# Attention pipeline of a decoder trunk: order of the copies and the scalings, and ScalarE making the upper half of each collected chunk

## What is computed

```python
s = jnp.einsum('bqhd,bkhd->bhqk', qi, k).astype(jnp.float32) * scale
p = masked_softmax(s, (kpos[None, :] <= qpos[:, None])[None, None])
return jnp.einsum('bhqk,bkhd->bqhd', p.astype(v.dtype), v)
...
out = gt[..., 0:1] * o_c + gt[..., 1:2] * o_s + gt[..., 2:3] * o_w
```

## Time and profile before

| what | us |
|---|---|
| median of the runs | 1398.74 |
| the profiled execution's own time | 1394.51 |
| its span, first to last instruction | 1392.5 |
| attention of the first layer | from about 141.5 to 251.8 |
| attention of the second layer | from about 773.4 to 882.6 |

### The profile page before, as it was taken

The page is one execution under the profiler, slowest core; times in us unless marked ns, Lnnn a source line. Parts: engine busy times, 40 slices in busy tenths (PEclk is TensorE's granted clock), DMA queues, the critical chain, the costliest instruction groups (busy, mean ns, idle before and its releaser), DMA issues.

```text
span 1392.5 us, 24791 instructions
## 1 busy us (share of the span) xinstructions
PE 1322.3 (95%) x10397; PEld 827.9 (59%) x10457; DVE 972.9 (70%) x1305; ACT 680.5 (49%) x970; POOL 151.9 (11%) x134
## 2 busy tenths in 40 slices
PE   7999898999999999999999989998999999999992
PEld 4357444444444444444356445458988988988981
DVE  7986676586650356334895675567888889989996
ACT  6245665253220132212245665347476677777772
POOL 0010331330000000031010120230400000000003
PEclk9999999999999999999999999999999999999997
DMA  8330883235320244003331100209899999999985
GB/s 314 106 91 16 275 295 116 98 130 180 138 91 0 96 176 167 1 16 141 127 91 31 31 1 1 65 14 369 319 376 373 339 357 393 369 369 391 364 312 198
DMA packets 39997, 255.49 MB, mean 183 GB/s; under 512 B 5626, under 2 KB 6778, under 8 KB 25418
## 3 DMA queue, kind: packets, MB, share of 16 engines
q1 hardware_dynamic: 30490, 220.00, 42.1%
q0 software_dynamic: 8960, 33.26, 7.2%
q10 hardware_dynamic: 432, 0.59, 0.1%
HBM read 218.08 MB, written 33.65 MB: 181 GB/s over the span
## 4 chain that ended last, share of the span: by engine, by line
PE 82%; issue 5%; DVE 5%; ACT 3%; DMA 3%; POOL 1%; SPq 0%; DVEq 0%; POOLq 0%; ACTq 0%
PE bank L1117 19%; PE bank L1118 19%; PE bank L1119 18%; PE bank L1338 4%; PE bank L1355 3%; PE bank L1385 2%; ACT arena L1655 2%; DVE small L2084 2%; PE bank L678 1%; PE bank L680 1%; PE bank L679 1%; PE bank L668 1%; PE bank L670 1%; PE bank L669 1%; DMA expert_slots<-arena,row_index 1%
## 5 line engine op out<-in xcount | busy, mean ns | idle before, releaser
L928 DVE SCALAR_TENSOR_TENSOR arena<-arena 128x3072 f16<-128x3072 f32 x86 | 288.3, 3352 | 11.0 <-ACT arena L782 10.9
L782 ACT ACTIVATE arena<-arena 128x3072 f16<-128x3072 f32 x86 | 237.9, 2767 | 42.2 <-DMA arena<-in_ew 23.3
L1117 PE MATMUL bank<-arena 128*128 128x144 bf16 (+3 forms) x893 | 218.9, 264 | 5.7 <-DVE arena L928 3.0
L1118 PE MATMUL bank<-arena 128*128 128x144 f16 (+3 forms) x894 | 219.2, 264 | 1.2 <-DVE arena L1842 1.2
L1119 PE MATMUL bank<-arena 128*128 128x144 bf16 (+3 forms) x883 | 215.0, 262 | 0.0
L1118 PE MATMUL bank<-hl,wring_hi 128*128 128x512 f16 x352 | 133.4, 379 | 1.4 <-issue 0.3
L1119 PE MATMUL bank<-hh,wring_lo 128*128 128x512 bf16 (+1 forms) x344 | 130.4, 379 | 0.0
L1117 PE MATMUL bank<-hh,arena 128*128 128x512 bf16 x337 | 127.7, 379 | 1.0
L1118 PE MATMUL bank<-hl,arena 128*128 128x512 f16 x338 | 128.1, 379 | 0.1
L1117 PE MATMUL bank<-hh,wring_hi 128*128 128x512 bf16 (+1 forms) x332 | 126.1, 380 | 0.6 <-DVE wring_lo L1792 0.3
L1119 PE MATMUL bank<-hh,arena 128*128 128x512 bf16 x319 | 120.9, 379 | 0.0
(11 more groups left out here) (333 smaller groups left out, 2637.5 us busy)
## 6 DMA issues: line engine op xcount, KB each, us to landing
arena<-in_ew SPq DMA_DIRECT2D x86, 1536.0 KB, 9.1
arena<-in_dw SPq DMA_DIRECT2D x22, 1536.0 KB, 6.8
wstage<-in_w_chunk SPq DMA_DIRECT2D x44, 512.0 KB, 3.6
expert_results<-iota POOLq DMA_DIRECT2D x9, 2048.0 KB, 20.9
arena<-in_cmp_w SPq DMA_DIRECT2D x2, 2048.0 KB, 9.8
expert_slots<-iota POOLq DMA_DIRECT2D x5, 512.0 KB, 18.2
expert_results<-wstage SPq DMA_DIRECT2D x5, 512.0 KB
arena<-in_w_tok SPq DMA_DIRECT2D x2, 1096.0 KB, 7.1
```

The costliest lines, as they stand in the source:

```text
L782: act.activation(ew_hi_[:, G % EP, :], ew[:, G % ES, :], ACT.Copy, scale=SW).then_inc(M["hi_ready"], 1)
L928: dve.scalar_tensor_tensor(out=ew_lo_[:, G % EP, :], in0=ew[:, G % ES, :], scalar=SW, in1=ew_hi_[:, G % EP, :], op0=ALU.mult, op1=ALU.subt ...
L1117: pe.matmul(out, w_hi, x_hi, start=first, stop=False)
L1118: pe.matmul(out, w_hi, x_lo, start=False, stop=False)
```

## The change

ScalarE issues the copy of step g-3 ahead of the exponentials of step g. VectorE issues the scaling of step g-2 ahead of the minimum of step g. The upper half of a collected chunk is written by ScalarE (an Activate with Copy and a scale) in the same rounds, behind the exponentials; VectorE drops its own and waits for ScalarE's before it writes the remainder.

```diff
@@ ScalarE
+                def collect_upper(u):
+                    chunk, opens, closes = pair_out(u)
+                    if closes:
+                        act.wait_ge(*ready("pv", l, u))
+                        act.activation(mixh[:, chunk, :], out_bank[chunk % 2][:, :], ACT.Copy,
+                                       scale=SX).then_inc(*signal("mix_hi", l, chunk))
+
                 for g in range(ND + 3):
+                    if g >= 3:
+                        turned(g - 3)
                     if g < ND:
                         exps(g)
                     if g == 2:
                         w_hi(NW * l + NF - 1 + WR)
                     if 0 <= g - TANH_DUO < LC:
                         gelu_tanh(g - TANH_DUO)
-                    if g >= 3:
-                        turned(g - 3)
+                    if g >= 3 * TT - 1 and g % TT == TT - 1:
+                        collect_upper((g + 1) // TT - 3)
+                collect_upper(NU - 2)
+                collect_upper(NU - 1)
@@ VectorE, keep
-                link(dve.tensor_scalar(mixh[:, chunk, :], src, SX, None, ALU.mult))
                 dve.scalar_tensor_tensor(out=mixl[:, chunk, :], in0=src, scalar=SX, in1=mixh[:, chunk, :],
                                          op0=ALU.mult, op1=ALU.subtract).then_inc(*signal(*label))
@@ VectorE, collect and its loop
                         dve.wait_ge(*ready("pv", l, u))
+                        dve.wait_ge(*ready("mix_hi", l, chunk))
                         keep(chunk, out_bank[chunk % 2][:, :], ("mix", l, chunk))
 
                 for g in range(ND + 2):
-                    if g < ND:
-                        maximum(g)
                     if g >= 2:
                         scale(g - 2)
                         scaled(2 * (g - 2))
                         scaled(2 * (g - 2) + 1)
+                    if g < ND:
+                        maximum(g)
```

## The result

The changed kernel takes 1376.81 us (median of four runs, 1376.59 to 1379.87), the one before 1398.76 us in its first four runs. The profiled execution took 1376.63 us, its span 1374.6 us; the profiled execution of before took 1394.5, so the two profiles differ by 17.9 us only.

A forecast was written before the change was run, and what follows sets the result against it. TensorE, busy 95% of the span, was taken as the bound, losing time in the two attentions. Terms 14.1 + 3.8 - 0.6 - 1.0 - 1.1 = 15.2 us, off the 1398.7 us median, gave 1383.5 us, range 1378.5 to 1391.

The forecast's parts named there:

- In the steady NSA part the waits removed are 5.1 us: Steady rounds of both attentions: TensorE's transposes stop waiting for ScalarE's copy, 14.1 us gained over NSA and MLA parts.
- the two ends: Round 35 on: new wait for the scaling costs 0.5 us a layer, a clock fall 1.1 us in the second.
- The start: First rounds of each attention: earlier copy removes a 1.50 us pause and its clock loss, 1.9 us a layer gained.
- the supposition: At each attention's start, a new 0.85 us pause does not cost the clock; otherwise 0.5 us each is left.
- The copy delaying the exponentials: Steady rounds: exponentials slip by up to 0.8 us behind the copy, hidden because scores need them two rounds later.
- The scaling ahead of the minimum, at nothing: VectorE's order: cost 0, hidden under the scores, bounds -0.3 to +0.3 us a round; brings no time by itself.
- The collections: VectorE waits for ScalarE's upper half: rounds 15 and 23 about 0, round 31 0.3 us, round 35 about 2.2 us new wait.
- part of it is given back: Rival: longer hops between engines make rounds 15, 23 and 31 cost TensorE about 1 us each; 1389.5 us, chance 0.13.
- the slower one: Rival: VectorE's wait behind `mix_hi` costs 3.3 us at each of 8 collections, 5 us slower, 1403.8 us; chance 0.04.
- The price of the upper half: ScalarE's 128x512 copy in a collection costs about 0.585 us, bounds 0.37 and 1.05, and frees 0.69 us of VectorE.
- The clock at the end: Behind round 35's new wait the clock falls in both layers: first as before, second loses 1.1 us.
- more comes: Rival: clock never falls at the end, or ends overlap better; gain 19 to 23 us, 1377.5 us, chance 0.10.

The follow-up runs named there:

- after_again: The changed kernel, unedited, profiled once more: 1382.06 us in one run, attentions 202.2 us.
- copy_scaling: Kernel before with ScalarE's copy ahead of the exponentials and VectorE's scaling ahead of the minimum, VectorE still making both halves: 1369.97 us, ratio 0.9804.
- copy_only: Kernel before with only ScalarE's copy moved ahead of the exponentials: 1375.94 us, ratio 0.9852 to before.
- upper_early: Changed kernel with ScalarE writing the upper half ahead of the round's exponentials, behind the copy: 1369.76 us, ratio 0.9794 to before.

## Why the prediction was wrong, point by point

The mechanism and the new waits came as worked out; the sum was 15.2 us where the attentions gave 20.7. The step that failed is "In the steady NSA part the waits removed are 5.1 us ... and 5.2 us ...; in the MLA part 1.9 us each ... Sum 14.1 us": a term that was mis-sized. With the 0.6 us of round 31's collections taken off it was 13.5 us, and it measured 18.0. The other terms came near: the two starts 3.8 us and measured 4.1, the two ends -2.1 and measured -1.4. So 4.5 of the 5.5 us between sum and attentions are this term.

- **The steady part.** From mask 5 to mask 35 the prediction had 7.0 - 0.3 = 6.7 us in layer 1 and 6.8 in layer 2. The table gives 6.71 + 2.88 = 9.59 and 7.00 + 2.75 = 9.75. Of this, the half-clock time behind the start's pause that reaches beyond mask 5 (at 152.36 and 784.46 us) belongs to the start. Windows of before:

```profile
152.00:154.00 2.00, 2.00 (x9) 1.18 (x8) 1.17 (x3) 0.78 (x4) 1.89 (x2) 0.50 1.01 330
...
783.00:785.00 2.00, 2.00 (x9) 0.85 (x8) 0.57 (x3) 0.91 (x3) 0.00 (x0) 0.50 0.78 242
785.00:787.00 2.00, 2.00 (x12) 1.15 (x10) 1.66 (x4) 1.39 (x5) 0.00 (x0) 0.86 0.05 20
```

  In layer 1 that is 1.64 x 0.5 = 0.8 us, in layer 2 0.54 x 0.5 + 2 x 0.14 = 0.55 us. That leaves 8.8 and 9.2 us: 2.1 and 2.4 us more than the prediction had. The windows from mask 5 to mask 35 show where it lies, first before, then after, layer 1 and 2:

```profile
152.36:237.86 85.50, 78.47 (x465) 40.21 (x464) 56.17 (x126) 52.88 (x152) 20.81 (x24) 0.99 0.76 254
784.46:869.79 85.33, 78.08 (x465) 39.87 (x464) 56.04 (x126) 52.67 (x152) 9.98 (x10) 0.99 0.01 3
...
151.55:227.46 75.91, 75.60 (x464) 39.69 (x464) 57.02 (x129) 55.44 (x159) 21.92 (x25) 1.00 0.88 291
771.39:846.96 75.57, 75.27 (x463) 39.19 (x463) 53.51 (x127) 55.35 (x159) 9.86 (x10) 1.00 0.02 7
```

  TensorE's idle time fell by 6.7 and 7.0 us, nearly what was predicted. Its busy time fell too, by 2.9 and 2.8 us, with the same matmuls (one or two records are missing); the clock is 0.8 and 0.55 us of that, and 2.1 and 2.3 us remain. A reason fits the rows. An idle row counts from the modelled end of the last matmul, and a matmul that need not wait starts before that end. After an unhindered mask the transposes start 0.12 us behind its start (159.93, 160.05), its row lasts 0.28 us, and in the earlier trace rows the transposes began 0.70 us behind the row's end. So each wait costs its idle row and 0.16 us; 13 waits in layer 1 and 12 in layer 2 make 2.1 and 1.9 us. This is worked out from the rows and agrees in size with both layers' busy time; no run tried it alone.
- **The start.** Predicted 1.9 us a layer. To mask 5 it gave 1.07 and 1.62 us, with the clock's share behind it 1.9 and 2.2. Right in the pair of profiles that I compare, though in layer 1 not one pause of 0.85 us came, but 0.27, 0.16 and 0.27 us, 0.7 in all. In after_again the clock fell at the first start all the same (0.52 and 0.63 over 8 us, 3.4 us lost). In the profiles of all kernels with the copy in front it stayed up at 17 starts of 18, and with the copy behind it fell at all 8. So the supposition holds in nearly every start, but not in all.
- **The copy delaying the exponentials.** Right: hidden everywhere in the steady part (0.5 us of delay in round 8 with no one waiting).
- **The scaling ahead of the minimum, at nothing.** Right only for the order alone, which gained nothing. With the copy in front it is worth 6 us (copy_scaling against copy_only), by which the copy order alone is held back in rounds where a scaling is behind a minimum, above all where it runs beside GpSimd. "It brings no time by itself" was true, and I did not price what it brings to the other part.
- **The collections.** By the idle rows rounds 15 and 23 cost nothing, round 31 0.2 us (predicted 0.3), round 35 1.99 us (predicted 2.2), each in both layers. Against copy_scaling, which has no such wait, round 15 costs 0.16 and 0.50 us (masks 17 to 18: 2.47 and 2.81 us against 2.31), round 23 nothing and round 31 0.42 us in each layer (masks 33 to 34: 3.27 against 2.85). So a wait that is shorter than the overlap, or that stands between a step's two heads, shows in no idle row. The rival "part of it is given back" and the slower one fell with it. The release does come from VectorE standing behind `mix_hi`: upper_early took only that wait away.
- **The price of the upper half.** Predicted 0.585 us and measured 0.59 to 0.60 (L1672, 12 of them). The estimate from the page "ScalarE: Activation LUTs" of the Trainium skill, section "Rules for kernel authors", was 0.72 us; the trace is 0.12 us below it. The row there gives its 0.3 us for an Activate whose bias is a pointer, and this one is given none in the kernel, so the row was not the right one to work from. Its advice, to leave multiplications to VectorE, no run here bears out: ScalarE takes 0.60 us where VectorE took 0.69, and upper_early and copy_scaling differ by 0.2 us.
- **The clock at the end.** Predicted to fall in each layer. In four ends of the changed kernel it fell in three (15.44, 15.23 and 13.95 us against 13.09 without); in four ends of before it had fallen in two (14.15 and 13.94, against 13.03 and 12.80). The means differ by 0.95 us an end, 1.9 us in all, where I had 2.1. Right as a mean. In the pair of profiles that I compare the total came near by luck: the clock stayed up in the first layer, where I had let it fall, and the second lost 2.4 us, where I had 1.6.
- **Against the median.** I worked the sum out from one profiled execution, 4.2 us below the median, and took it from the median. The changed kernel's profiled execution was at its own median. Outside the attentions executions differ by 6.7 us, which nothing in the change touches. Of the 6.7 us between forecast and median 5.5 are the terms above; 1.3 us, with rounding, are such differences.
- **The clock and small pauses.** The page "TensorE: Matmul & The Clock Gate" of the Trainium skill, section "A second HAM failure mode: psum-queue depth-cycling", would have put the time below my sum, and there it came out, but not for its reason: in the steady part of before, some 13 pauses of up to 0.95 us a layer, the clock was at 1.00 once it was back from the start's fall, and so it was in the steady parts of all thirteen profiles. The one case for the page is the start of after_again, where it fell with no pause over 0.27 us.

The time fell in the rival "more comes", for which I had 19 to 23 us and a chance of 0.10. Its grounds did not come: the clock fell at three ends of four, and in the profiles compared the two ends together lost 1.4 us. It also took idle time plus clock for an upper bound, and the waits' real price lies above their idle time. So its number is right by luck.

## What to carry to other kernels

On engines that work in order, put work that is ready and that the bottleneck waits for ahead of work that still waits for a result; then go through what stands behind every new wait, as the upper half behind the exponentials, which cost 7 us by its place alone, 2.4 of them through the clock in the profiled execution. Look also at what else runs beside the work that is to be early: a scaling beside GpSimd took 2.19 us here where it took 0.62 alone, and the order with time to spare hid it. When a wait of TensorE goes, count its idle row plus what the next matmul would have overlapped with the last, here 0.16 us a wait. Set a sum from one profiled execution against several, since the parts that no one touches differ by more than small terms.

## What was unexpected about the hardware

Idle rows behind a matmul understate a wait (0.12 us from start to start where the row lasts 0.28). The clock fell behind pauses of 1.5 to 2.1 us in most attentions and not in others of the same kernel: at the start behind 1.50 us each time, at the end behind 1.70 us in 4 of 8 and behind 1.99 us in 3 of 4. Behind the same 1.99 us the end took 13.09 us with the clock at 1.00, or up to 15.44 us with part of it at 1.2 GHz. Behind the pauses of up to 0.96 us in the steady part it never fell, nor behind 1.34 us at an end, and yet it fell once at a start whose longest pause was 0.27 us. What decides it these runs leave open. VectorE's scalings of 128x256 took 0.41 us alone and up to 1.46 us beside GpSimd's instructions.
